# Attention masks as bf16 products on TensorE; maxima and exponentials read from PSUM

## The chip, the cores and the metric

One core of a Trainium2 chip runs the whole program. The metric is device time in microseconds (us); lower is better. The engines are TensorE (PE in the profile, its weight loads PEld), VectorE (DVE), ScalarE (ACT), GpSimd (POOL) and SyncE (SP), which issues most transfers. Matrix products write to PSUM, 8 banks of 512 fp32 numbers for each of 128 partitions.

## The reference

Three blocks of width 1024 run over one sequence of 256 tokens in fp32: sparse attention with a feed-forward part, a gated linear recurrence (HGRN) with one, and a block with gated linear attention and latent attention side by side, then a third feed-forward part. The change touches two softmaxes.

```python
# block 1: 16 heads of 64; each query keeps its best 64 keys
score = jnp.where(causal[None], score, -jnp.inf)
_, sel = lax.top_k(score, topk)
valid = sel <= t_pos[None, :, None]
logits = jnp.einsum('bqgrd,bqkgd->bqgrk', qg, k_sel) * (ATT_HEAD_DIM ** -0.5)
logits = jnp.where(valid[:, :, None, None, :], logits, -jnp.inf)
p = jax.nn.softmax(logits, axis=-1)
o = jnp.einsum('bqgrk,bqkgd->bqgrd', p, v_sel)
...
# block 3: 8 heads of 128 + 64 (rope)
s = jnp.where(mask[None, None], s, -jnp.inf)
p = jax.nn.softmax(s, axis=-1)
return jnp.einsum('bhqk,bkhd->bqhd', p, v)
```

## The kernel before

Weights come as 168 tiles of 128x2048 fp32 through a ring of six (`load`, L322, on SyncE). ScalarE rounds each to a high half (`hi`, L330), GpSimd subtracts to get the low half (`lo`, L334), and TensorE multiplies high and low halves in three passes (`mm3`, L350 to L352). A tile's place is free for the next load when TensorE has used it. ScalarE splits tiles between its other work, in the order that the code gives (`hi_until`); it splits none while it runs the attention loop.

Both attention stages use the same three loops, one for each engine: `attend_pe`, `attend_act`, `attend_dve`. They work on pairs of heads: eight pairs in the 16-head stage (`dsa_pe`), four in the 8-head stage (`mla_pe`). The logits of one head are 128x384: queries 0 to 127 against 128 keys, and queries 128 to 255 against all 256. The two heads of pair i lie in PSUM banks 2(i mod 2) and 2(i mod 2)+1, so that two pairs have room. For a pair:

- TensorE computes the logits (`logits`: L677, L678 in the 16-head stage; L1839, L1841 in the 8-head one). All these products have fp32 operands.
- VectorE adds the mask while it copies both heads from PSUM to the SBUF buffer `lg[i % 3]` (L761, 128x768), which frees the banks (`lg_free`). Then it takes the maxima (L767, L768) and multiplies them by minus the scale (L771).
- ScalarE applies the exponential in place in `lg`, four passes with sums (L736).
- VectorE takes reciprocals (L777) and normalises (L783).
- TensorE transposes six blocks (L721) to banks 4 and 5; ScalarE copies them to `pts` (L744); TensorE multiplies by the values (L685 to L687, or L1849 to L1851) into bank 6 or 7; ScalarE and VectorE split the output into a high and a low half (L858 and L951, or L1897 and L1951).

Every engine runs its instructions in the order of the code and waits on semaphores. TensorE's order is: logits of pairs 0 and 1; then for each i: wait for `lg_free` of pair i, logits of pair i+2, wait for the normalised pair i (`pn_ready`), transposes of pair i, value products of pair i-1. ScalarE's: exponentials 0 and 1; then copy i, output i-1, exponentials i+2. VectorE's: mask addition and maxima of i+2, normalise i+1, output half of i-1.

The mask of the 16-head stage, `sbias`, is made by VectorE after the selection of the best keys (L941, L946); the logits of pairs 0 and 1 are computed while that selection runs. The mask of the 8-head stage, `mbias`, is a constant that GpSimd writes in the setup (L409 to L412).

## Time and profile before

| | us |
|---|---|
| median of 3 runs | 1232.85 (1232.03 to 1233.91) |
| profiled execution | 1234.36 |
| its span, first to last instruction | 1232.2 |
| TensorE busy | 1112.5 (90%) |
| GpSimd busy | 829.6 (67%) |
| ScalarE busy | 551.1 (45%) |
| VectorE busy | 471.4 (38%) |
| mask additions, L761: 8 of 0.947 and 4 of 0.956 | 11.4 |
| mean granted clock of TensorE | 0.956 |

A busy share is a mean over stages that have different limits, so the timelines of the two stages tell more than the table. A timeline row gives start, duration, engine, line, operation and operands; [x <- y] is idle time before it and what ended that. The granted clock is 1.00 for TensorE's 2.4 GHz and 0.50 for 1.2 GHz. An fp32 product shows as two records.

### The profile page before, as it was taken

Reading aid. Unit: us, or ns where it says so; the run is one execution under the profiler, and the core shown is the slowest. Engines: PE = TensorE matmul, PEld = TensorE weight load, DVE = VectorE, ACT = ScalarE, POOL = GpSimd, SP = SyncE. Lnnn points to the kernel's source line nnn. Section 1 sums busy time; section 2 is a strip of 40 time slices with the busy share of each in tenths; the row PEclk is TensorE's granted clock in tenths of the full one; section 3 lists DMA queues with packets and bytes.
Section 4 is the critical chain, followed back from the end, with each engine's and each line's share of the span. In section 5 each row is a group of like instructions: output and inputs, shape, how many; then the busy total and the mean of one; then the engine's idle time right before and its main releaser. Section 6 shows DMA issues by size and latency. Waiting matters only on the chain.

```text
span 1232.2 us, 15620 instructions
## 1 busy us (share of the span) xinstructions
PE 1112.5 (90%) x6548; PEld 961.9 (78%) x6548; DVE 471.4 (38%) x854; ACT 551.1 (45%) x742; POOL 829.6 (67%) x299
## 2 busy tenths in 40 slices
PE   4675999999999966599999998999988898999997
PEld 4564787888889964477888888999988797788886
DVE  7559531114450779952111023260127525111102
ACT  3354544444335455444443425455563533543430
POOL 5243249978849757546987956978486274798880
PEclk9876999999999986699999999999998999999999
DMA  7210165555446530046555544554434143655540
GB/s 260 104 57 1 38 255 189 199 174 182 160 164 234 184 104 1 2 158 230 176 191 185 176 170 155 183 178 165 144 130 171 46 161 137 222 188 187 176 166 35
DMA packets 27952, 185.88 MB, mean 151 GB/s; under 512 B 3630, under 2 KB 4060, under 8 KB 6380
## 3 DMA queue, kind: packets, MB, share of 16 engines
q1 hardware_dynamic: 26156, 178.60, 41.2%
q10 hardware_dynamic: 1728, 6.29, 1.5%
q8 instruction: 52, 0.85, 0.3%
q14 instruction: 16, 0.13, 0.0%
HBM read 183.83 MB, written 1.05 MB: 150 GB/s over the span
## 4 chain that ended last, share of the span: by engine, by line
PE 78%; DVE 14%; ACT 3%; POOL 2%; issue 1%; DMA 1%; DVEq 0%
PE ps L350 24%; PE ps L352 24%; PE ps L351 24%; POOL wl L334 2%; DVE arena L1448 2%; DVE arena L468 1%; DVE arena L1449 1%; ACT wh L330 1%; PE ps L1114 1%; PE ps L1841 1%; DVE arena L1463 1%; PE ps L979 1%; DMA stage<-in_tiles 1%; DVE arena L783 1%; DVE arena L924 1%
## 5 line engine op out<-in xcount | busy, mean ns | idle before, releaser
L334 POOL TENSOR_TENSOR wl<-stage,wh 128x2048 fp32r<-128x2048 f32 x168 | 773.9, 4636 | 306.9 <-ACT wh L330 306.8
L330 ACT ACTIVATE wh<-stage 128x2048 fp32r<-128x2048 f32 x168 | 319.1, 1911 | 95.3 <-DMA stage<-in_tiles 94.3
L350 PE MATMUL ps<-wh,xh 128*128 128x512 f32 (+1 forms) x808 | 306.9, 380 | 18.2 <-POOL wl L334 5.9
L352 PE MATMUL ps<-wh,xl 128*128 128x512 f32 (+1 forms) x808 | 301.2, 373 | 0.0
L351 PE MATMUL ps<-wl,xh 128*128 128x512 f32 (+1 forms) x808 | 301.0, 372 | 0.0
L350 PEld LDWEIGHTS ps<-wh,xh 128*128 128x128 f32 x808 | 155.3, 192 | 48.4 <-issue 5.7
L350 PE MATMUL ps<-xh,wh 128*128 128x256 f32 x628 | 180.0, 287 | 8.6 <-DVE xl L1911 4.1
L351 PE MATMUL ps<-xl,wh 128*128 128x256 f32 x628 | 178.8, 285 | 0.0
L352 PE MATMUL ps<-xh,wl 128*128 128x256 f32 x628 | 178.7, 285 | 0.0
L352 PEld LDWEIGHTS ps<-wh,xl 128*128 128x128 f32 x808 | 155.2, 192 | 26.1
L351 PEld LDWEIGHTS ps<-wl,xh 128*128 128x128 f32 x808 | 155.6, 193 | 24.7 <-issue 0.5
L350 PEld LDWEIGHTS ps<-xh,wh 128*128 128x128 f32 x628 | 121.6, 194 | 10.7 <-DVE xl L1911 4.3
L1205 DVE TENSOR_TENSOR arena<-arena,ps 128x256 f32<-128x256 f32 x66 | 27.8, 421 | 251.3 <-ACT arena L1182 251.3
L351 PEld LDWEIGHTS ps<-xl,wh 128*128 128x128 f32 x628 | 121.7, 194 | 0.1
L352 PEld LDWEIGHTS ps<-xh,wl 128*128 128x128 f32 x628 | 121.7, 194 | 0.0
L350 PE MATMUL ps<-wh,hh 128*128 128x512 f32 x296 | 117.7, 398 | 0.0
L351 PE MATMUL ps<-wl,hh 128*128 128x512 f32 x296 | 117.0, 395 | 0.0
L352 PE MATMUL ps<-wh,hl 128*128 128x512 f32 x296 | 117.0, 395 | 0.0
L1182 ACT ACTIVATE arena<-ps 128x256 f32<-128x256 f32 x66 | 25.3, 383 | 186.9 <-PE ps L352 186.8
L352 PEld LDWEIGHTS ps<-wh,hl 128*128 128x128 f32 x296 | 55.6, 188 | 13.4
L351 PEld LDWEIGHTS ps<-wl,hh 128*128 128x128 f32 x296 | 55.6, 188 | 13.1
L350 PEld LDWEIGHTS ps<-wh,hh 128*128 128x128 f32 x296 | 55.6, 188 | 13.1
(338 smaller groups left out, 1136.9 us busy)
## 6 DMA issues: line engine op xcount, KB each, us to landing
stage<-in_tiles SPq DMA_DIRECT2D x168, 1024.0 KB, 4.9
arena<-in_ln_g ACTq DMA_DIRECT2D x4, 512.0 KB, 3.5
arena<-in_ln_b ACTq DMA_DIRECT2D x4, 512.0 KB, 4.7
x_res<-in_x SPq DMA_DIRECT2D x1, 1024.0 KB, 5.1
out<-x_res SPq DMA_DIRECT2D x4, 256.0 KB, 2.0
arena<-in_pre_mix_norm ACTq DMA_DIRECT2D x1, 512.0 KB, 7.9
arena<-in_post_mix_norm ACTq DMA_DIRECT2D x1, 512.0 KB, 3.7
arena<-in_pre_ffn_norm ACTq DMA_DIRECT2D x1, 512.0 KB, 5.0
```

The costliest lines, as they stand in the source:

```text
L330: nc.scalar.activation(wh[:, ring(n), :], stage[:, ring(n), :], ACT.Copy).then_inc(hi_done, 1)
L334: nc.gpsimd.tensor_tensor(wl[:, ring(n), :], stage[:, ring(n), :], wh[:, ring(n), :].bitcast(F32), ALU.subtract).then_inc(lo_done, 1)
L350: mm(out_, lh, rh, start=start, stop=False, skip_group_check=skip)
L351: mm(out_, lh, rl, start=False, stop=False, skip_group_check=skip)
L352: return mm(out_, ll, rh, start=False, stop=stop, skip_group_check=skip)
L468: V.scalar_tensor_tensor(out=x, in0=n, scalar=-part, in1=x, op0=ALU.mult, op1=ALU.add).then_inc(dve_step.sem, dve_step.up())
L783: ins = V.tensor_scalar(x, x, small[:, w:w + 1], None, ALU.mult)
L924: V.scalar_tensor_tensor(out=score[:, c0:c1], in0=x, scalar=w, in1=score[:, c0:c1], op0=ALU.mult, op1=ALU.add).then_inc(scored.sem, scored ...
L979: last = nc.tensor.transpose(ps[:, bank + b, k * P:(k + 1) * P], src[:, t, c:c + P], ident[:])
L1182: nc.scalar.activation(silu_g[:, p % 2, t, :], ps[:, pair_bank(G, p, t), 0:256], ACT.Silu).then_inc(s_done.sem, s_done.up())
L1205: V.tensor_tensor(hp[:, p % 2, t, :], silu_g[:, p % 2, t, :], ps[:, pair_bank(G, p, t), 256:512], ALU.mult).then_inc(h_mul.sem, h_mul.up())
L1448: V.tensor_tensor(y[:, :, 0:d], k_[:, :, 0:d], e[:, :, 0:d], ALU.mult)
```

## The change

The masks `mbias` and `sbias` become bf16, and GpSimd writes a bf16 copy of the identity matrix, `identb`, in the setup. The logits are no longer closed sums: TensorE adds the mask to them in PSUM as a product of `identb` and the mask (`masked` in `attend_pe`), four products for a pair of heads. `attend_dve` loses the mask addition; its maxima are read from PSUM. ScalarE's exponentials read PSUM and write `lg`. The semaphore `lg_free` is gone. TensorE's logits of pair i+2 wait for `p_ready`, the end of the exponentials of pair i. The logits of pairs 0 and 1 are both issued ahead of the first mask; in the 16-head stage TensorE waits for `sbias` between them and the masks.

```diff
@@ -177,8 +177,9 @@
-        mbias = sb("mbias", [P, 3 * P])
-        sbias = sb("sbias", [P, 3 * P])
+        mbias = sb("mbias", [P, 3 * P], BF16)
+        sbias = sb("sbias", [P, 3 * P], BF16)
+        identb = sb("identb", [P, P], BF16)
@@ -402,6 +403,8 @@
+            pool.wait_ge(consts.sem, consts.now())
+            nc.gpsimd.tensor_copy(identb[:], ident[:])
@@ -674,9 +677,9 @@
-                    mm(ps[:, b, 0:P], qt[:, i, 0:P], kpad[:, gr, e, 0:P], start=True, stop=True)
-                    last = mm(ps[:, b, P:3 * P], qt[:, i, P:T], kpad[:, gr, e, :], start=True, stop=True)
-                return last
+                    mm(ps[:, b, 0:P], qt[:, i, 0:P], kpad[:, gr, e, 0:P], start=True, stop=False, skip_group_check=True)
+                    mm(ps[:, b, P:3 * P], qt[:, i, P:T], kpad[:, gr, e, :], start=False, stop=False,
+                       skip_group_check=True)
@@ -686,7 +689,10 @@
-            attend_pe(pe, HEADS // 2, logits, weighted)
+            logits(0)
+            logits(1)
+            pe.wait_ge(sel_done.sem, sel_done.due(pe, 2))
+            attend_pe(pe, HEADS // 2, logits, sbias, weighted)
@@ -696,7 +702,14 @@
-        def attend_pe(pe, pairs, logits, weighted):
+        def attend_pe(pe, pairs, logits, bias, weighted):
+            def masked(i):
+                for e in range(2):
+                    b = 2 * (i % 2) + e
+                    mm(ps[:, b, 0:P], identb[:], bias[:, 0:P], start=False, stop=True, skip_group_check=True)
+                    last = mm(ps[:, b, P:3 * P], identb[:], bias[:, P:3 * P], start=False, stop=True, skip_group_check=True)
+                last.then_inc(lg_ps.sem, lg_ps.up())
+
@@ -707,11 +720,12 @@
             for i in range(2):
-                logits(i).then_inc(lg_ps.sem, lg_ps.up())
+                masked(i)
             for i in range(pairs):
                 if i + 2 < pairs:
-                    pe.wait_ge(lg_free.sem, lg_free.due(pe))
-                    logits(i + 2).then_inc(lg_ps.sem, lg_ps.up())
+                    pe.wait_ge(p_ready.sem, p_ready.due(pe))
+                    logits(i + 2)
+                    masked(i + 2)
@@ -732,8 +746,8 @@
-                        x = lg[i % 3][:, e, c0:c1]
-                        ins = nc.scalar.activation(x, x, ACT.Exp, bias=small[:, at + 4:at + 5], scale=scale,
+                        x, y = lg[i % 3][:, e, c0:c1], ps[:, 2 * (i % 2) + e, c0:c1]
+                        ins = nc.scalar.activation(x, y, ACT.Exp, bias=small[:, at + 4:at + 5], scale=scale,
@@ -751,17 +765,10 @@
-        def attend_dve(dve, pairs, scale, bias, outputs):
-            def masked(i):
+        def attend_dve(dve, pairs, scale, outputs):
+            def largest(i):
                 dve.wait_ge(lg_ps.sem, lg_ps.due(dve))
-                x = lg[i % 3]
-                if i >= 3:
-
-                    dve.wait_ge(pt_ps.sem, pt_ps.seen(dve) + i - 2)
-                V.tensor_tensor(x, ps[:, 2 * (i % 2):2 * (i % 2) + 2, 0:3 * P],
-                                bias.unsqueeze(1).to_broadcast([P, 2, 3 * P]), ALU.add
-                ).then_inc(lg_free.sem, lg_free.up())
-                dve.wait_ge(lg_free.sem, lg_free.now())
+                x = ps[:, 2 * (i % 2):2 * (i % 2) + 2, 0:3 * P]
...
@@ -1850,7 +1856,9 @@
-            attend_pe(pe, MH // 2, logits, weighted)
+            logits(0)
+            logits(1)
+            attend_pe(pe, MH // 2, logits, mbias, weighted)
```

In `mla_pe` the three products of a logit block change their start and stop flags in the same way.

TensorE, 8-head stage, before, from the last logits of pair 1 to the transposes of pair 0 (L1839 and L1841 are the logits, L721 the transposes; `m_d`, `m_a` and the like are semaphores):

```order
L1839 MATMUL ps<-arena 128x256
L1841 MATMUL ps<-arena 128x256 x2
L1839 MATMUL ps<-arena 128x128 [waits lg_free]
L1841 MATMUL ps<-arena 128x128 x2
...
L721 MATMUL ps<-ident,arena 128x128 [waits pn_ready]
L721 MATMUL ps<-ident,arena 128x128 x5
```

The same place after (the logits are now L1845 and L1848, the masks L709 and L710, the transposes L735):

```order
L1845 MATMUL ps<-arena 128x256
L1848 MATMUL ps<-arena 128x256 x2
L709 MATMUL ps<-mbias,identb 128x128
L710 MATMUL ps<-mbias,identb 128x256
...
L1845 MATMUL ps<-arena 128x128 [waits p_ready]
L1848 MATMUL ps<-arena 128x128 x2
...
L709 MATMUL ps<-mbias,identb 128x128
L710 MATMUL ps<-mbias,identb 128x256
L735 MATMUL ps<-ident,arena 128x128 [waits pn_ready]
L735 MATMUL ps<-ident,arena 128x128 x5
```

The masks of pairs 0 and 1 (two rows twice for each pair) stand behind the logits of both, the logits of pair 2 wait for `p_ready` instead of `lg_free`, and their masks stand between them and the transposes of pair 0. In the 16-head stage the order is the same, with a wait for `sel_done` at the first mask.

VectorE, 16-head stage, one turn of its loop before (L761 mask addition, L767 and L768 maxima, L777 reciprocals, L783 normalising):

```order
L761 TENSOR_TENSOR arena<-ps,sbias 128x768 [waits lg_ps]
L767 TENSOR_REDUCE small<-arena 128x2 [waits lg_free]
L768 TENSOR_REDUCE small<-arena 128x2
L771 TENSOR_SCALAR small<-small 128x4 [waits dve_step]
L777 RECIPROCAL small<-small 128x4 [waits p_ready]
L783 TENSOR_SCALAR arena<-arena,small 128x128 [waits dve_step]
```

And after:

```order
L774 TENSOR_REDUCE small<-ps 128x2 [waits lg_ps]
L775 TENSOR_REDUCE small<-ps 128x2
L778 TENSOR_SCALAR small<-small 128x4 [waits dve_step]
L784 RECIPROCAL small<-small 128x4 [waits p_ready]
L790 TENSOR_SCALAR arena<-arena,small 128x128 [waits dve_step]
```

The addition is gone, the maxima read PSUM and wait for TensorE's masks themselves, and the rest keeps its order.

## Rows read from the trace of the kernel before

**Rows 1.** Page, chain that ended last, by engine, as shares of the span.

```profile
PE 78%; DVE 14%; ACT 3%; POOL 2%; issue 1%; DMA 1%; DVEq 0%
```

**Rows 2.** Timeline, VectorE, one period, 16 heads: start, duration, [idle before].

```profile
122.03 0.95 DVE L761 TENSOR_TENSOR arena<-ps,sbias 128x768 f32<-128x768 f32 x1
123.02 0.42 DVE L767 TENSOR_REDUCE small<-arena 128x2 f32<-128x256 f32 x1
...
125.60 0.95 DVE L761 TENSOR_TENSOR arena<-ps,sbias 128x768 f32<-128x768 f32 x1
```

**Rows 3.** Timeline, TensorE, the same period.

```profile
122.64 0.43 PE L685 MATMUL ps<-arena 128*64 128x128 f32 x2
...
123.72 0.49 PE L677 MATMUL ps<-arena 128*128 128x128 f32 x2
124.04 0.60 PE L678 MATMUL ps<-arena 128*128 128x256 f32 x2
...
124.70 0.60 PE L678 MATMUL ps<-arena 128*128 128x256 f32 x2
125.41 0.87 PE L721 MATMUL ps<-ident,arena 128*128 128x128 f32 x6
126.21 0.43 PE L685 MATMUL ps<-arena 128*64 128x128 f32 x2
```

**Rows 4.** Timeline, TensorE, head of the 16-head attention.

```profile
106.57 0.80 PE L677 MATMUL ps<-arena 128*128 128x128 f32 x2 [12.39 <-DVE arena L761]
...
108.44 1.06 PE L678 MATMUL ps<-arena 128*128 128x256 f32 x2
111.05 1.54 PE L721 MATMUL ps<-ident,arena 128*128 128x128 f32 x6 [1.55 <-DVE arena L783]
...
114.68 0.82 PE L721 MATMUL ps<-ident,arena 128*128 128x128 f32 x6
```

**Rows 5.** Timeline, ScalarE, its first exponential.

```profile
107.80 0.40 ACT L736 ACTIVATE arena<-arena,small 128x128 f32<-128x128 f32 x1 [19.11 <-DVE small L771]
```

**Rows 6.** Chain that ended last, end of the 16-head attention: start, us, what.

```profile
131.40 1.87 ACT arena L736 x8
```

**Rows 7.** Timeline, TensorE, the 8-head attention.

```profile
957.65 0.46 PE L1839 MATMUL ps<-arena 128*128 128x128 f32 x2 [2.07 <-DVE small L1948]
...
965.59 0.38 PE L1839 MATMUL ps<-arena 128*128 128x128 f32 x2
...
974.10 0.82 PE L721 MATMUL ps<-ident,arena 128*128 128x128 f32 x6
...
979.95 0.87 PE L721 MATMUL ps<-ident,arena 128*128 128x128 f32 x6
```

**Rows 8.** Timeline, VectorE, first mask addition of the 8-head attention.

```profile
961.86 0.96 DVE L761 TENSOR_TENSOR arena<-ps,mbias 128x768 f32<-128x768 f32 x1 [4.35 <-PE ps L1841]
```

**Rows 9.** Timeline, ScalarE, first exponential of the 8-head attention.

```profile
964.10 0.40 ACT L736 ACTIVATE arena<-arena,small 128x128 f32<-128x128 f32 x1 [5.66 <-DVE small L771]
```

**Rows 10.** Timeline, TensorE, another wait.

```profile
51.81 0.47 PE L350 MATMUL ps<-wh,xh 128*128 128x512 f32 x1 [2.18 <-DVE xl L890]
```

**Rows 11.** Windows: length, busy us of each engine, granted clock, DMA share, GB/s.

```profile
53.00:56.30 3.30, 3.30 (x9) 2.54 (x8) 3.23 (x6) 0.35 (x1) 2.87 (x1) 0.50 0.22 92
926.80:933.50 6.70, 5.59 (x26) 5.59 (x27) 6.37 (x8) 0.09 (x1) 5.31 (x1) 0.50 0.16 66
```

**Rows 12.** Groups by form, ScalarE: busy us, mean ns; idle before.

```profile
L1182 ACT ACTIVATE arena<-ps 128x256 f32<-128x256 f32 x66 | 25.3, 383 | 186.9 <-PE ps L352 186.8
L1339 ACT ACTIVATE arena<-arena 128x256 f32<-128x256 f32 x48 | 20.0, 416 | 39.9 <-POOL arena L1408 39.9
```

**Rows 13.** Timeline, TensorE, neighbouring products of 256 columns.

```profile
985.25 0.27 PE L352 MATMUL ps<-xh,wl 128*128 128x256 f32 x1
985.37 0.28 PE L350 MATMUL ps<-xh,wh 128*128 128x256 f32 x1
```

**Rows 14.** Waits of TensorE: us in total, times, longest.

```profile
PE ps L350 <- POOL wl L334: 5.9, 6, 1.5
```

More of the change, by code:

```diff
@@ L291, in build @@
         q_rot, qt_ps, qt_done, sel_done = signals("q_rot qt_ps qt_done sel_done")
-        lg_ps, lg_free, nmx_ready, p_ready, pn_ready, pt_ps, pts_done, ot_ps, oh_done = signals(
-            "lg_ps lg_free nmx_ready p_ready pn_ready pt_ps pts_done ot_ps oh_done")
+        lg_ps, nmx_ready, p_ready, pn_ready, pt_ps, pts_done, ot_ps, oh_done = signals(
+            "lg_ps nmx_ready p_ready pn_ready pt_ps pts_done ot_ps oh_done")
         s_done, h_mul, h_ready = signals("s_done h_mul h_ready")
@@ L726, in attend_pe @@
             value(pairs - 1)
-            lg_free.skip(pe, 2)
+            p_ready.skip(pe, 2)
         def attend_act(act, pairs, scale, outputs):
@@ L784, in normalised @@
                 ins.then_inc(pn_ready.sem, pn_ready.up())
-            masked(0)
-            masked(1)
+            largest(0)
+            largest(1)
             normalised(0)
@@ L790, in attend_dve @@
                 if i + 2 < pairs:
-                    masked(i + 2)
+                    largest(i + 2)
                 if i + 1 < pairs:
@@ L796, in attend_dve @@
                     outputs(i - 1)
-            pt_ps.skip(dve, pairs)
             dve.wait_ge(oh_done.sem, oh_done.due(dve))
@@ L952, in outputs @@
                 ).then_inc(x_ready.sem, x_ready.up())
-            attend_dve(dve, HEADS // 2, HD ** -0.5, sbias[:], outputs)
+            attend_dve(dve, HEADS // 2, HD ** -0.5, outputs)
         def dsa_pool(pool):
@@ L1838, in logits @@
                         y = slice(t * P, (t + 1) * P)
-                        mm(ps[:, b, c0:c1], qn[:, h, y], kn[:, h, 0:c1 - c0], start=True, stop=False)
+                        mm(ps[:, b, c0:c1], qn[:, h, y], kn[:, h, 0:c1 - c0], start=t == 0, stop=False,
+                           skip_group_check=True)
                         for x in range(2):
-                            last = mm(ps[:, b, c0:c1], rr[:, x, h // 4, y], kp[x][:, h % 4, 0:c1 - c0],
-                                      start=False, stop=x == 1)
-                return last
+                            mm(ps[:, b, c0:c1], rr[:, x, h // 4, y], kp[x][:, h % 4, 0:c1 - c0],
+                               start=False, stop=False, skip_group_check=True)
             def weighted(i, e, pt, _):
@@ L1952, in outputs @@
                 ).then_inc(x_ready.sem, x_ready.up())
-            attend_dve(dve, MH // 2, (MN + MR) ** -0.5, mbias[:], outputs)
+            attend_dve(dve, MH // 2, (MN + MR) ** -0.5, outputs)
             dve.wait_ge(gates_done.sem, 4)
```

## The prediction

> **What bounds the kernel now.** I read three views in this order: the chain that ended last, then the timelines of the two attention stages engine by engine, then the granted clock around waits. The chain is TensorE for 78% of the span and VectorE for 14% [rows 1], so a VectorE instruction is worth something only in a stage where the chain runs over VectorE. The change touches two short stages: the 16-head attention (about 105.6 to 138.4 us) and the 8-head one (957.65 to about 984.9).
>
> In the **16-head stage** VectorE sets the pace. One pair of heads is one turn of its loop: from one mask addition (L761) to the next is 125.60 - 122.03 = 3.57 us, and the addition holds 0.99 of it, up to the start of the maxima [rows 2]. TensorE is close behind. Its turn is the value products (122.64 to 123.72, 1.08 us), the logits of the pair two further on (123.72, their last row ends at 124.70 + 0.60 = 125.30), and the six transposes (125.41 to 126.21, 0.80) [rows 3]. Records overlap: the row at 123.72 is 0.49 long and the next starts at 124.04, 0.17 before its end. With as much behind the last one, TensorE's own work is 1.08 + 1.41 + 0.80 = 3.29 us of the 3.57.
>
> In the **8-head stage** TensorE sets the pace up to the second group of transposes: the logits of the first two pairs run from 957.65 to 965.59, 3.97 us a pair, and those of the third pair follow without a pause [rows 7]. Behind 974.10 the chain goes over ScalarE (copy, output, exponentials) and VectorE to the last transposes at 979.95 [rows 7].
>
> **The change part by part.**
>
> *Mask addition on VectorE, removed.* 12 instructions of 0.95 us. In the 16-head stage six of them stand in the steady loop: VectorE's turn falls from 3.57 to 2.58 us. In the 8-head stage only the first one (961.86) is on the way to the exponentials [rows 8].
>
> *Masks on TensorE, added.* Each pair gets four bf16 products, 128, 256, 128 and 256 columns. The trace has no bf16 product. Neighbouring single-pass products of 256 columns start 0.12 us apart [rows 13]; a 128-column one cannot cost more than that and hardly less than half. A pair costs 2 x (0.06 + 0.12) = 0.36 to 4 x 0.12 = 0.48; I take 0.40, since every one also loads the identity. At the half clock I take 0.80. The Trainium skill ("TensorE: Matmul & The Clock Gate", section "Wait — 56ns, not 53.3ns?") measures 55.6 ns for 128 bf16 columns. By it a pair would cost about 0.33 us, an estimate, and the six masks on the path would be 0.4 us cheaper together.
>
> *Maxima and exponentials out of PSUM.* A ScalarE pass over 128x256 takes 383 ns from PSUM and 416 from SBUF, of different functions [rows 12]. I take 0.03 us less for each of four exponentials in a pair, 0.13 a pair, with bounds 0 and 0.4. L761 reads PSUM and takes 0.95 us for 768 elements, no more per element than the maxima out of SBUF (0.42 for 256) [rows 2], so the maxima stay the same; bounds -0.05 and +0.15 a pair. The Trainium skill ("VectorE: DVE Perf Modes", section on the TRN2 errata) gives VectorE a fixed term of 58 cycles from SBUF and 120 from PSUM. That would be 0.13 us more for the two maxima of a pair, a rule against this change; the row of L761 shows nothing of it, and the sum would move by under 0.3 us.
>
> *The wait that is exchanged.* This is the heart of it. Before, TensorE's logits of pair i+2 wait for the mask addition of pair i, which empties the bank. Now the bank is read by the exponentials, and the wait is for them. What queues behind it on TensorE, in order: those logits, their masks, the transposes of pair i, and the value products.
>
> 8-head stage. The masks of pair 0 now stand behind the logits of both first pairs. So pair 0's maxima start not at 962.85 (961.86 plus 0.99 [rows 8]) but at 965.59 + 0.40 (its masks) + 0.2 (time to the end of the last product) = 966.2. That is 3.35 later, and the first exponential moves from 964.10 [rows 9] to 967.45. The pair's exponentials take 1.87 us [rows 6], so they end at 969.3. Logits of pair 2 start at 969.36 instead of 965.59: +3.77. Two masks on the way to the second transposes add 0.80. Second transposes: 974.10 + 4.57 = 978.67. Behind them the order is unchanged, over ScalarE, and the mask of the last pair is already done; the third transposes have over a microsecond of room. Less 0.13 for the exponentials of the first pair and of the last: **+4.3 us**.
>
> 16-head stage, head. Logits of two pairs lie ready long before; only their masks wait for the selection. TensorE had been idle for 12.39 us and is slow: six transposes take 1.54 us where they take 0.87 later [rows 3, 4]. The masks of pair 0, 0.80 plus 0.2, end where the addition ended (106.57 [rows 4]), so the first exponential stays at 107.80 [rows 5]: removed and added work cancel. But logits of pair 2, which filled TensorE's idle time from 106.57 to 109.50 [rows 4], now wait for the exponentials, 107.80 + 1.87 = 109.7. They then need 2.6 at the slow clock and their masks 0.80: first transposes at 113.1 instead of 111.05, ended at 114.4. Logits 1.41 and masks 0.40 at full clock: second transposes at 116.3 instead of 114.68 [rows 4], +1.6. If the clock rises sooner, because TensorE now works without a pause from 109.7, it is +0.9. I take +1.4.
>
> 16-head stage, loop. TensorE's turn is 3.29 + 0.40 = 3.69 against 3.57. VectorE has 2.6, so TensorE now sets the pace. The way over ScalarE is shorter: transposes to value products 0.80, to the output 1.19, to the exponentials 0.44, these 1.87, less the 0.91 from the next transposes to their copy, makes 3.4. Four turns: **+0.5** (bounds +0.2 and +1.4). From the sixth transposes on the end runs over ScalarE as before, through the last pair's exponentials at 131.40 [rows 6]: -0.1. Stage sum 1.4 + 0.5 - 0.1 = **+1.8**.
>
> *The clock.* In the 8-head stage TensorE now stands idle from about 966.2 to 969.36, 3.2 us. A wait of 2.18 us at 49.6 [rows 10] was followed by 3.3 us at clock 0.50 with TensorE busy throughout; behind a longer one TensorE was busy 5.59 us of a stretch at 0.50 [rows 11]. The wait of 2.07 us before 957.65 [rows 7] brought no fall. Half of the busy time is lost: 1.7 or 2.8 us. The logits behind the gap are all on the path. I take **+2.0**.
>
> *Setup.* GpSimd copies the identity once to bf16, and waits once for it; it stands idle for 9 us before its first weight tile, so this costs nothing. If it were not hidden it would be 0.5 us.
>
> Sum: 4.3 + 1.8 + 2.0 = 8.1 us. The profiled execution took 1234.36 us (span 1232.2), 1.5 above the median of 1232.85; it would become 1242.5, and the median **1241.0**. What follows either stage is work released by its last output, on all engines, so the delay arrives whole at the end.
>
> **Rivals.**
> *The clock does not fall.* For it: the wait of 2.07 us. Against: the wait of 2.18 us, and this one is 3.2. Sum 6.1: 1239.0.
> *Bf16 masks cost TensorE more than any row shows*, through changes between fp32 and bf16 or weight loads that are not hidden, 0.8 a pair. Nothing in the trace speaks for it. Twice the mask cost on eight masks of the path is +3.2: 1244.2.
> *The delay is taken up behind the 8-head stage* (the other side). If the weight pipeline set the pace there, a later start would only shorten TensorE's waits for it. The 6.3 us of that stage vanish, and +1.8 is left, 1234.7, within what counts as no change. It decides only if TensorE then waits over 6 us for low halves of weights; all such waits together are 5.9 us, the longest 1.5 [rows 14], and the splitting on ScalarE is queued behind the attention, so it starts later too.
> *VectorE's freed time carries through*: if masks cost TensorE nothing, the turn is 3.4 by ScalarE, four turns give -0.7, and the stage ends at +0.6; the rest stays: 1239.8. It lies inside the range.
>
> **How the numbers follow.** Forecast with the fall of the clock 0.60, no fall 0.24, dearer masks 0.08, taken up behind 0.05, the freed time 0.03. The range: low end with no fall, head +0.9 and cheap exponentials, 4.0 + 1.0 = 5.0, so 1237.5; high end with the clock at 2.8, head 1.6, loop +1.4 and masks at 0.48, about 11.5, so 1244.5. A measurement of this kernel tells 0.2% (2.5 us) from no change. Slower by more: 0.92. Within: 0.06, nearly all from the fourth case. Faster: 0.02.
>
> **What the profile after would show.** A gap on TensorE of about 3.2 us behind the first two masks of the 8-head stage, ended by the exponentials of ScalarE; clock 0.50 behind it; second transposes 4.6 us later than before, or more by the clock. In the 16-head stage the logits of pair 2 start near 109.7, transposes come 3.7 us apart and VectorE has idle time in each turn. The prediction is wrong if transposes come under 3.5 us apart, if that gap is under 2 us, or if the end of a stage moves and the span does not.

## The result

Before: 1233.03 us, median of 6 (1231.87 to 1233.99). After: 1237.35 us, median of 6 (1236.75 to 1239.8). The ratio is 1.0036, 95% interval 1.0026 to 1.0047: the changed kernel is 4.3 us slower. The direction was forecast, the size was not: 1241.0 was predicted, with a range from 1237.5, and the median lies just under it. One execution further on, in experiment two, took 6107.85 us, and the ratio there leaves it out.

The profiled execution of after took 1239.8 us (span 1237.5), the slowest of its six. Against the profiled execution of before (1234.36) that is 5.4 us. All of it lies in the two attention stages:

| stretch of the two traces | before | after |
|---|---|---|
| start to the mask `sbias` | 105.52 | 105.50 |
| `sbias` to the next weight product | 32.90 | 34.14 |
| from there to the first logits of the 8-head stage | 819.23 | 819.09 |
| 8-head stage, to the weight product behind it | 27.26 | 31.46 |
| from there to the end of the span | 247.3 | 247.3 |

So the 16-head stage cost 1.2 us, the 8-head stage 4.2, and nothing was taken up behind either. The setup, 105.50 us to the mask against 105.52, cost nothing, as forecast.

The page of after, its busy times and its chain by engine (the chain answers to [rows 1]):

```profile
PE 1111.2 (90%) x6596; PEld 962.1 (78%) x6596; DVE 460.6 (37%) x842; ACT 547.9 (44%) x742; POOL 829.6 (67%) x300
...
PE 78%; DVE 13%; ACT 4%; POOL 3%; issue 1%; DMA 0%; DVEq 0%
```

VectorE is busy for 10.8 us less than before (471.4), and the kernel is slower: VectorE went down in the chain by a single percent.

The timeline of TensorE in the head of the 16-head stage of after (start, duration, operation, [idle before <- what ended it]; it answers to [rows 4]). L709 and L710 are the masks, L680 and L681 the logits, L735 the transposes:

```profile
105.56 0.29 PE L709 MATMUL ps<-sbias,identb 128*128 128x128 bf16 x1 [11.15 <-DVE sbias L952]
105.64 0.42 PE L710 MATMUL ps<-sbias,identb 128*128 128x256 bf16 x1
...
109.51 0.80 PE L680 MATMUL ps<-arena 128*128 128x128 f32 x2 [2.50 <-ACT arena L750]
...
112.88 1.49 PE L735 MATMUL ps<-ident,arena 128*128 128x128 f32 x6
...
116.29 0.82 PE L735 MATMUL ps<-ident,arena 128*128 128x128 f32 x6
```

The logits of pair 2 start 2.9 us later than before (106.57): they wait for ScalarE's exponentials. At half the clock they and their masks need 3.37 us up to the transposes (109.51 to 112.88).

One turn of the steady loop of after, TensorE (it answers to [rows 3]):

```profile
119.86 0.82 PE L735 MATMUL ps<-ident,arena 128*128 128x128 f32 x6
...
121.68 0.49 PE L680 MATMUL ps<-arena 128*128 128x128 f32 x2
...
123.10 0.22 PE L709 MATMUL ps<-sbias,identb 128*128 128x128 bf16 x1
123.15 0.27 PE L710 MATMUL ps<-sbias,identb 128*128 128x256 bf16 x1
123.26 0.22 PE L709 MATMUL ps<-sbias,identb 128*128 128x128 bf16 x1
...
123.43 0.82 PE L735 MATMUL ps<-ident,arena 128*128 128x128 f32 x6
```

A turn is 123.43 - 119.86 = 3.57 us, to the hundredth what it was before, when VectorE set it. It is now TensorE's own work without a pause: 1.82 (transposes and value products), 1.42 (logits), 0.33 (four masks, 123.10 to 123.43). In the same turn VectorE (it answers to [rows 2]) waits for the masks:

```profile
120.06 0.42 DVE L774 TENSOR_REDUCE small<-ps 128x2 f32<-128x256 f32 x1 [0.89 <-PE ps L710]
120.40 0.68 DVE L775 TENSOR_REDUCE small<-ps 128x2 f32<-128x512 f32 x1
```

That 0.89 us of idle time is what became of the 0.99 us of the mask addition. The maxima take from PSUM what they took from SBUF (0.42).

The 8-head stage of after, TensorE (it answers to [rows 7]); L1845 and L1848 are the logits:

```profile
958.73 0.46 PE L1845 MATMUL ps<-arena 128*128 128x128 f32 x2 [2.07 <-DVE small L1956]
...
966.67 0.22 PE L709 MATMUL ps<-mbias,identb 128*128 128x128 bf16 x1
...
970.23 0.49 PE L1845 MATMUL ps<-arena 128*128 128x128 f32 x2 [2.74 <-ACT arena L750]
...
979.51 0.82 PE L735 MATMUL ps<-ident,arena 128*128 128x128 f32 x6
```

and ScalarE's first exponential, which answers to [rows 9]:

```profile
968.46 0.37 ACT L750 ACTIVATE arena<-ps,small 128x128 f32<-128x128 f32 x1 [8.94 <-DVE small L778]
```

From the first logits to the second transposes it is 20.78 us, before 16.45. The two masks' products of pair 0 stand behind the logits of both pairs, the first exponential comes 9.73 us after the stage's start instead of 6.45, and TensorE stands for 2.74 us. Behind it TensorE runs at full clock: from the first transposes to the second it is 979.51 - 974.60 = 4.91 us, 0.65 for the transposes, 3.93 for a pair's logits and 0.33 for its masks.

### The profile page after: what moved, and what is told of

It is laid out like the page before. It is cut to its first block, busy times and chain, and to the rows that moved or that the text cites. A ratio compares the mean times of both kernels' runs of the same rounds, so it can differ in the third digit from the quotient of the medians.

```text
span 1237.5 us, 15699 instructions
## 1 busy us (share of the span) xinstructions
PE 1111.2 (90%) x6596; PEld 962.1 (78%) x6596; DVE 460.6 (37%) x842; ACT 547.9 (44%) x742; POOL 829.6 (67%) x300
## 4 chain that ended last, share of the span: by engine, by line
PE 78%; DVE 13%; ACT 4%; POOL 3%; issue 1%; DMA 0%; DVEq 0%
PE ps L351 24%; PE ps L353 23%; PE ps L352 23%; POOL wl L335 3%; DVE arena L1454 2%; DVE arena L471 1%; DVE arena L1455 1%; ACT wh L331 1%; PE ps L1120 1%; PE ps L1848 1%; DVE arena L1469 1%; PE ps L735 1%; PE ps L985 1%; ACT arena L750 1%; PE ps L681 1%
## 5 line engine op out<-in xcount | busy, mean ns | idle before, releaser
L353 PEld LDWEIGHTS ps<-wh,hl 128*128 128x128 f32 x296 | 55.6, 188 | 13.4
L352 PEld LDWEIGHTS ps<-wl,hh 128*128 128x128 f32 x296 | 55.6, 188 | 13.1
L351 PEld LDWEIGHTS ps<-wh,hh 128*128 128x128 f32 x296 | 55.6, 188 | 13.1
```

Of the source, the lines that this page charges most:

```text
L351: mm(out_, lh, rh, start=start, stop=False, skip_group_check=skip)
L352: mm(out_, lh, rl, start=False, stop=False, skip_group_check=skip)
L353: return mm(out_, ll, rh, start=False, stop=stop, skip_group_check=skip)
```

## The experiments

Ratios are against the kernel before, run on the same chip in the same series, with 95% intervals; its medians there were 1233.37 (one to four), 1233.96 (five to eight), 1234.01 (nine to twelve) and 1234.13 us (thirteen to fifteen). A ratio is not the quotient of the medians: a few long executions move it and not them. The theory that they test (A): the loss is the exchanged wait and the place of the masks behind both pairs' logits, in two places, plus a slow clock of TensorE that may or may not follow the gap. What a trace shows of single stretches is one execution; the medians are over 5 to 12.

**One: where the masks of pair 0 stand.** The changed kernel, but in the 8-head stage the masks of a pair follow that pair's logits, so those of pair 0 come ahead of the logits of pair 1.

```
             logits(0)
+            masked(0)
             logits(1)
-            masked(0)
             masked(1)
```

> The changed kernel, but in the 8-head stage the masks of pair 0 stand right behind the logits of pair 0, ahead of those of pair 1. Theory A (the order of the masks behind both logit blocks makes the wait for the exponentials visible; nothing else costs much in this stage): pair 0's exponentials end about 965 to 966 relative to a stage start of 957.65, before TensorE is through with pair 1, so the gap of 2.7 us is gone; from the stage's first product to the second transposes 16.45 + 4 x 0.33 = 17.8 us against 20.8 in the changed kernel; time 3.0 us below the changed kernel, about 1.3 above the kernel before. Rival B (the exchanged wait itself costs, wherever the masks stand): a gap of over 1 us stays, and the time is less than 1.5 us below the changed kernel.

Measured: 1234.61 us, median of 12; ratio 1.0016 (1.0004 to 1.0028). Its TensorE timeline in the 8-head stage:

```profile
972.65 0.27 PE L713 MATMUL ps<-mbias,identb 128*128 128x256 bf16 x1
972.76 0.39 PE L1887 MATMUL ps<-arena 128*128 128x128 f32 x2
```

The masks of pair 1 end and the logits of pair 2 follow without a gap: the exponentials of pair 0 are done in time. From the first logits to the second transposes the trace has 19.44 us. Of these 1.67 are a slow clock at the start of the stage, behind the wait of 2.05 us ahead of it; the first logits to the first transposes take 14.52 us, where in before, with three pairs' masks added, they would take 12.85. Less that it is 17.77, against 20.78 in after and 17.8 expected: the place of the masks is worth 3.0 us in the trace. In time it is 3.1 us by the medians (1.2 over before instead of 4.3) and some 2.3 by the ratios, in which the longest execution weighs. So the order of four small products cost several times what their execution does. The profiled execution was that longest one, 1242.23 us; the rest of its loss lies ahead of the stage, of the kind shown at thirteen below.

**Two and three: one stage at a time.** Two has the change in the 16-head stage alone, three in the 8-head stage alone; the other stage keeps VectorE's fp32 masks and the old wait.

> The change in the 16-head stage alone; the 8-head stage as before, with its fp32 mask and the addition on VectorE. Theory A (the stages add up, as their spans in the two traces say): +1.2 us against the kernel before, +0.2 to +1.5 depending on when the clock rises at the head of the stage, and 4.2 below the changed kernel. Rival B (in most executions the head of this stage gains, since TensorE is at full clock earlier than in the profiled one, and the measured 4.3 us are the 8-head stage alone): 0.0 or below.

> The change in the 8-head stage alone; the 16-head stage as before, with its fp32 mask and the addition on VectorE. Theory A: +4.2 us against the kernel before. If the clock fell behind the gap in most executions, as forecast: +6. If the delay were taken up behind the stage: under +1.

Measured: two 1233.97 us, ratio 1.0003 (0.9994 to 1.0012), with the stage 1.2 us longer in its trace (34.13), so the interval holds both no loss and the 1.2 us that were expected; three 1241.81 us, ratio 1.0059 (1.0045 to 1.0073). Three is slower than the whole change. Its trace, in windows (length, busy us of each engine, granted clock, DMA share, GB/s):

```profile
958.10:961.50 3.40, 3.40 (x12) 2.86 (x12) 0.00 (x0) 0.08 (x1) 3.24 (x1) 0.51 0.41 171
961.50:970.50 9.00, 6.32 (x42) 5.50 (x41) 2.28 (x6) 1.71 (x9) 1.25 (x1) 1.00 0.00 0
971.70:975.10 3.40, 3.40 (x13) 2.96 (x12) 0.07 (x1) 0.42 (x2) 0.00 (x0) 0.50 0.00 0
```

The clock fell twice to 1.2 GHz (0.50), with TensorE busy throughout: once behind the wait of 2.07 us ahead of the stage, once behind the 2.74 us gap. The stage took 34.80 us, which is 31.46 and twice 1.67. That accounts for this trace. Why the median of three lies over that of the whole change, which has the same gap, is not shown.

**Four and seven: the gap filled.** Twelve unread fp32 products of 128 columns into bank 4 behind the masks of pairs 0 and 1; four is the whole change so filled, seven the 8-head stage alone.

```
+            for _ in range(12):
+                mm(ps[:, 4, 0:P], ident[:], ident[:], start=True, stop=True)
```

> The changed kernel with twelve fp32 products of 128 columns (identity by identity, into bank 4, read by nobody) in the gap of the 8-head stage, so that TensorE is busy for 2.6 of its 2.7 us. If the clock falls behind the gap in most executions (the forecast), this takes away 1.7 to 2.8 us. If it does not fall, as in the profiled execution of the changed kernel: within 0.3 us of it.

> The change in the 8-head stage alone, with twelve fp32 products that nobody reads in its gap. Theory C (the clock falls behind the 2.7 us gap in many executions, each time for 3.4 us or more): 1 to 2.5 us below the kernel that changes the 8-head stage alone, so about +5 against the kernel before. Rival D (the clock is the same with and without the gap): no difference to it.

Measured: four 1237.73 us, ratio 1.0038 (1.0025 to 1.0051), the same as the changed kernel; its trace shows the filler and the second transposes at 20.78 us, as in after:

```profile
964.95 2.84 PE L753 MATMUL ps<-ident 128*128 128x128 f32 x24
967.86 0.49 PE L1887 MATMUL ps<-arena 128*128 128x128 f32 x2
```

Seven 1238.49 us, ratio 1.0031 (1.0019 to 1.0043): 0.0028 or 3.4 us under three. The filler takes nothing away in the whole change, and in the 8-head stage alone as much as two falls cost. But it stands behind only one of three's two waits: the fall ahead of the stage it cannot have prevented, and seven's trace has none there either. So the 3.4 us are not shown to be the filler's alone.

**Five: TensorE kept warm ahead of the 16-head stage, first try.** Three unread products after each of seven rounds of the selection, and twelve behind the first masks.

> The changed kernel, with products nobody reads on TensorE in the 16-head stage: three fp32 products of 128 columns after each of seven rounds of the selection, and twelve in the wait behind the first masks. TensorE then has its full clock at the first mask. Theory A (the +1.6 us at the head of this stage is the slow clock under the logits of pair 2, which now stand on the path): first mask to second transposes 7.9 us instead of 10.7, and the time 2.8 us below the changed kernel. Rival (the head is set by the exponentials, not by the clock): under 1 us.

Measured: 1237.35 us, ratio 1.0048 (1.0028 to 1.0068), in two groups of executions, about 1236.7 and 1244. The trace shows that it didn't do what was meant:

```profile
91.25 4.85 PE L690 MATMUL ps<-ident 128*128 128x128 f32 x42
102.78 0.29 PE L715 MATMUL ps<-sbias,identb 128*128 128x128 bf16 x1 [6.68 <-DVE sbias L1000]
```

The first products were used up by 96.1, TensorE then stood for 6.7 us, and the masks ran at half clock as before. The twelve behind them brought the full clock for the logits of pair 2 and held these up by their own length; from the first mask to the second transposes it is 10.05 us instead of 10.73, where 7.9 was expected. The question is left to nine.

**Six: the exchanged wait alone.** The kernel before, masks in fp32 on VectorE, but TensorE's logits of pair i+2 wait for the exponentials of pair i.

```
-                    pe.wait_ge(lg_free.sem, lg_free.due(pe))
+                    pe.wait_ge(p_ready.sem, p_ready.due(pe))
```

> The kernel before with the exchanged wait alone: masks in fp32 and added by VectorE, but TensorE's logits of pair i+2 wait for the exponentials of pair i instead of the mask addition, in both stages. Theory A (the wait alone is nearly hidden in the 8-head stage, where TensorE works on pair 1 until 0.4 us before the exponentials of pair 0 end; what costs there is that the masks of pair 0 stand behind the logits of pair 1): +0.4 us from the 8-head stage and +0.4 from the head of the 16-head one, together +0.8 against the kernel before. Rival B (the wait itself is the loss): +3 or more.

Measured: 1234.13 us, ratio 1.0003 (0.9995 to 1.0012). In its trace the 16-head stage is 34.00 us long (before 32.90) and the 8-head stage 27.79 (27.26):

```profile
109.44 0.79 PE L681 MATMUL ps<-arena 128*128 128x128 f32 x2 [15.28 <-ACT arena L787]
...
966.78 0.49 PE L1890 MATMUL ps<-arena 128*128 128x128 f32 x2 [0.26 <-ACT arena L787]
```

The wait alone makes nearly the whole 1.2 us of the 16-head stage, in the head, and an eighth of the 8-head stage's 4.2. There the masks' place makes the rest, as experiment one says from the other side.

**Eight: the changed kernel once more.**

> The changed kernel itself, beside these. Theory A without a fall of the clock: 5.4 us above the kernel before, as the spans of the two stages say (1.2 and 4.2). With a fall behind the gap in most executions, 6 to 7.5 above. 4.3, as measured first, if the head of the 16-head stage costs less in most executions than in the profiled one. The trace shows which stretch of the 8-head stage has which clock.

Measured: 1238.58 us, ratio 1.0034 (1.0021 to 1.0047). This time its trace has the fall that was predicted, behind the same 2.74 us gap (windows, as above, both behind the gap):

```profile
968.50:971.90 3.40, 3.40 (x13) 2.99 (x13) 0.02 (x1) 0.38 (x2) 0.00 (x0) 0.54 0.00 0
972.00:980.00 8.00, 8.00 (x59) 7.29 (x59) 3.74 (x13) 3.23 (x10) 0.00 (x0) 0.99 0.01 2
```

The second transposes come at 22.45 us instead of 20.78: one fall costs 1.67 us. Seven traces have the gap unfilled (after, three, five, eight, and nine, thirteen and fourteen below); four show the fall (three, eight, thirteen, fourteen), and the second transposes then come 1.67 us later each time. The two with the filler show none. The wait of 2.0 to 2.07 us ahead of the stage was unfilled in fourteen traces, and the clock fell behind it in three (one, three and fifteen), again for 1.67 us each time.

**Nine: the 16-head stage at full clock.** The changed kernel; behind the logits of pairs 0 and 1 TensorE computes 30 unread products, waits for the first part of `sbias`, computes 17 more, and 10 behind the masks.

> The changed kernel, and TensorE no longer rests while the selection of the 16-head stage runs: behind the logits of pairs 0 and 1 it computes 30 unread fp32 products of 128 columns into bank 4, waits for the first part of sbias, computes 17 more, and 10 more behind the masks of pairs 0 and 1. Theory A (the price of the head of the 16-head stage is the slow clock under work that was moved behind sbias): at full clock the masks of pair 0, the logits of pair 2, their masks and the first transposes take 0.33 + 1.41 + 0.33 + 0.87 us instead of 0.64 + 2.6 + 0.64 + 1.54, so from the first mask to the second transposes it is about 8.2 us instead of 10.7, and the kernel lies 2.5 us under the changed kernel: 1.8 over before, ratio 1.0015. Rival B (ScalarE and VectorE set the head once the logits wait for the exponentials): under 1 us is gained, ratio 1.0030.

Its TensorE timeline:

```profile
105.30 0.23 PE L716 MATMUL ps<-sbias,identb 128*128 128x128 bf16 x1 [0.59 <-DVE sbias L1001]
...
108.95 0.49 PE L681 MATMUL ps<-arena 128*128 128x128 f32 x2 [0.58 <-ACT arena L791]
...
110.69 0.82 PE L774 MATMUL ps<-ident,arena 128*128 128x128 f32 x6
...
113.30 0.88 PE L774 MATMUL ps<-ident,arena 128*128 128x128 f32 x6
```

From the first mask to the second transposes it is 8.00 us, against 10.73 in after; 8.2 was expected. The stage takes 31.46 us, 2.7 less than after and 1.4 less than before. For the stage theory A holds: the price of its head is the slow clock. It does not show that TensorE is the better place for the masks, since before's head is at half clock; eleven below, which fills the same wait with the masks on VectorE, has 32.96 us, but its clock falls again behind a wait of 2.90 us ahead of the first transposes. The time does not follow: three executions took 1235.7 to 1236.2 us (1.1 to 2.9 under the changed kernel's two medians, 1237.35 and 1238.58), four took 1242.3 to 1244.1; median 1242.29, ratio 1.0049 (1.0027 to 1.0072). No execution of the kernel before (82) or of the changed kernel (11) took over 1240 us; 1 of 12 did in one, 4 of 9 in five and 4 of 7 here.

**Thirteen and fourteen: traces of the slower executions of nine.** The same kernel, twice.

> The kernel of e9_full_clock_16 once more, for the trace alone. Its seven executions fell into two groups, three of 1235.7 to 1236.2 us and four of 1242.3 to 1244.1, at the same mean clock (0.958 to 0.961); only one of the first group has a trace. Theory A (with a waiting TensorE kept busy the stage itself takes its 8.0 us from the first mask to the second transposes, and the 6 to 8 us come in at another place): in a slow execution the 16-head stage is again about 31.4 us long and the whole difference lies outside it. Rival B (the unread products outlast the wait for sbias in some executions and hold the masks up): the stage itself is 6 us or more longer.

> The same kernel as e13_full_clock_again, for a second chance of a trace from the slower group. Expected as there.

They took 1243.27 and 1250.57 us. In thirteen the 16-head stage is 31.45 us long, as in nine, and the loss is in the third block, ahead of the 8-head stage (825.27 us between the stages instead of 818.47), as theory A of that expectation said. The timeline of all engines at the same place, of nine and then of thirteen (DVE is VectorE; POOL L336 is GpSimd's splitting of weight tiles):

```profile
939.23 0.69 DVE L1994 TENSOR_TENSOR arena<-arena 128x512 f32<-128x512 f32 x1
939.61 4.79 POOL L336 TENSOR_TENSOR wl<-stage,wh 128x2048 fp32r<-128x2048 f32 x1 [9.66 <-ACT wh L332]
939.95 4.47 DVE L1996 COPY small<-small 128x2 f32<-128x2 f32 x1
```

```profile
937.69 9.52 POOL L336 TENSOR_TENSOR wl<-stage,wh 128x2048 fp32r<-128x2048 f32 x2 [8.46 <-ACT wh L332]
937.77 0.69 DVE L1992 TENSOR_TENSOR arena<-ps,trig_t 128x512 f32<-128x512 f32 x1
938.50 4.36 DVE L1994 TENSOR_TENSOR arena<-arena 128x512 f32<-128x512 f32 x1
...
942.89 4.34 DVE L1996 COPY small<-small 128x2 f32<-128x2 f32 x1
```

In nine GpSimd started at 939.61, when L1994 was already running, and one VectorE instruction was held. In thirteen it started at 937.69, ahead of L1994, and two in a row were held, 4.36 and 4.34 us, where they take 0.69 and 0.17 (0.17 is that copy in fifteen's trace). L1992, which reads PSUM, was not. TensorE then waited:

```profile
947.29 0.80 PE L352 MATMUL ps<-wh,xh 128*128 128x512 f32 x1 [5.34 <-DVE small L1996]
```

5.34 us instead of 0.61, and its clock fell to 0.50 behind that. Why GpSimd started sooner shows some 15 us ahead, at the wait of [rows 11], here of nine and then of thirteen:

```profile
925.58 0.58 PE L352 MATMUL ps<-xh,wh 128*128 128x256 f32 x1 [4.16 <-DVE xl L1967]
```

```profile
924.36 0.39 PE L352 MATMUL ps<-xh,wh 128*128 128x256 f32 x1 [2.89 <-DVE xl L1967]
```

In nine GpSimd was still splitting tiles when L1967 (two inputs from SBUF) began, and it took 2.76 us; in thirteen the tiles were done, and it took 1.49. TensorE then waited 2.89 us instead of 4.16, its mean clock in the 6.7 us from 924.4 was 0.75 instead of 0.54 (from 924.5), the next tiles came sooner, and so did the collision. All three traces of long executions (one, thirteen, fourteen) have the wait of 2.89 us; the other eleven traces with this wait unfilled, before's and after's among them, have 4.12 to 4.16. So in the traces the shorter executions are those in which TensorE waits longer here. Ten, below, has the same by experiment. In fourteen the same happened, and besides the other rival came true: the selection ended with `sbias` ready at 105.04, while the 17 unread products stood ahead of the masks:

```profile
104.63 6.70 PE L691 MATMUL ps<-ident 128*128 128x128 f32 x34 [4.27 <-DVE sbias L996]
111.16 0.22 PE L716 MATMUL ps<-sbias,identb 128*128 128x128 bf16 x1
```

Here the two instructions that write `sbias` came behind each other in 0.8 us, after GpSimd's tiles; in after and in nine they were held for 4.0 and 4.6 us. The filler was sized for that case and delayed the masks by 6.1 us.

**Ten to twelve: waits filled in the kernel before.** Ten: 16 unread products in the wait of 4.13 us behind which the clock is 0.50 [rows 11], and 8 in the wait ahead of the 8-head stage. Eleven: also the products of nine. Twelve: also the masks of pairs 3, 5 and 7 of the 16-head stage on TensorE.

> The kernel before, masks on VectorE, with unread products in two waits of TensorE in the third block: 16 fp32 products of 128 columns in the wait of 4.13 us at 923.8, and 8 in the wait of 2.07 us ahead of the 8-head attention. Theory A (the granted clock falls behind a wait of TensorE and not by itself): the 6.7 us at clock 0.50 from 926.8, in which TensorE is busy for 5.59, become full clock and give back 2.8 us: ratio 0.9977, about 1230.6. Rival B (the clock falls there whatever TensorE does, or what follows is bound by the splitting of weights): nothing is gained, ratio 1.000; products that outlast the wait cost up to 1 us.

> As e10_two_waits_filled, and the products of e9_full_clock_16 in the wait for the selection too (30, 17, and 4 behind the logits of pair 1), masks on VectorE. Theory A (slow clock in the head of the 16-head stage costs the kernel before something too): the first transposes take 0.87 instead of 1.54 us, and the second ones come 0.7 to 1.5 us sooner: ratio 0.9968. Rival B: VectorE's mask additions set the head, 0.3 us or less is gained: 0.9975.

> As e11_all_filled, and the masks of pairs 3, 5 and 7 of the 16-head stage come from TensorE in bf16 (maxima and exponentials of these pairs from PSUM), all others from VectorE; the 8-head stage keeps its fp32 masks on VectorE. Theory A (before, the loop is VectorE's with 3.57 us a pair; with all masks on TensorE it is TensorE's with 3.57; shared, neither has them all): TensorE has 3.29 and 3.62 us in turn, so the transposes come 3.4 to 3.5 us apart and some 0.5 us are gained: ratio 0.9964. Rival B (the wait for the exponentials, exchanged for these pairs, costs TensorE what VectorE gains): no gain, 0.9968 or more.

Measured: 1237.35, 1237.4 and 1237.16 us; ratios 1.0029 (1.0019 to 1.0039), 1.0030 (1.0019 to 1.0041), 1.0038 (1.0023 to 1.0053). All three lose where a gain was expected, and the trace of ten tells why. First the wait that it fills and the next one, in before:

```profile
927.91 0.58 PE L350 MATMUL ps<-xh,wh 128*128 128x256 f32 x1 [4.13 <-DVE xl L1911]
...
946.92 0.50 PE L350 MATMUL ps<-wh,xh 128*128 128x512 f32 x1 [0.44 <-DVE small L1940]
```

Then ten:

```profile
926.80:933.50 6.70, 6.70 (x58) 6.70 (x57) 6.06 (x9) 0.01 (x1) 2.19 (x1) 1.00 0.46 157
...
943.70:950.60 6.90, 4.36 (x10) 3.46 (x11) 2.49 (x1) 0.00 (x0) 2.46 (x1) 0.51 0.01 2
```

```profile
946.24 0.79 PE L352 MATMUL ps<-wh,xh 128*128 128x512 f32 x1 [5.59 <-DVE small L1997]
```

The first row is the stretch of [rows 11]: the clock is 1.00 now. But TensorE's next tiles came sooner, GpSimd started its pair of tiles sooner (936.40), and VectorE's same two instructions fell behind it (3.55 and 4.34 us). TensorE waited 5.59 us where it had waited 0.44, and the slow clock came there. Up to the start of that wait 2.7 us were gained (805.39 us behind the 16-head stage instead of 808.06), and more was given back, 4.5 us net between the stages. Eleven and twelve have the same wait, 5.56 and 5.61 us. Eleven's own question, whether the slow clock in the head of the 16-head stage costs the kernel before something too, got no clean answer: its second transposes come 9.16 us after `sbias`, as in before, with the clock fallen again.

**Fifteen: masks shared.** The kernel before, and the masks of pairs 3, 5 and 7 of the 16-head stage on TensorE.

> The kernel before, and the masks of pairs 3, 5 and 7 of the 16-head stage from TensorE in bf16, their maxima and exponentials from PSUM; all other masks on VectorE, no unread products. Theory A (the loop is bound by VectorE before and by TensorE with all masks there; shared it is bound by neither all the time, as the trace of e12_all_filled_mixed shows with transposes 3.29 and 3.59 us apart in turn): stage 0.5 us shorter than before's 31.85 from the logits of pair 2 to the next weight product, time 0.5 us under before, ratio 0.9996, which such a measurement cannot tell from 1. Rival B (the gain in e12 hangs on the filled wait): stage 31.8 or longer, ratio 1.0000 or more.

Measured: 1233.16 us, median of 12, beside 1234.13 for before; ratio 0.9999 (0.9986 to 1.0012), no change. Its TensorE timeline:

```profile
113.38 0.82 PE L770 MATMUL ps<-ident,arena 128*128 128x128 f32 x6
116.62 0.82 PE L770 MATMUL ps<-ident,arena 128*128 128x128 f32 x6
120.20 0.87 PE L770 MATMUL ps<-ident,arena 128*128 128x128 f32 x6
123.50 0.82 PE L770 MATMUL ps<-ident,arena 128*128 128x128 f32 x6
```

The transposes come 3.24, 3.58 and 3.30 us apart instead of 3.57. From the second transposes to the next weight product it is 22.85 us against 23.74, 0.9 less; 0.6 of that goes in the first interval (4.23 instead of 3.63), where the masks of pair 3 run in the cold head. What is left, 0.3 us, no such measurement can tell. Of the versions with masks on TensorE this one and two cannot be told from before; none is faster.

## Why the prediction was right and where it failed

*8-head stage, +4.3.* The forecast held: +4.33 at the second transposes, +4.20 at the stage's end. Its three parts held as well: masks behind both pairs' logits, ScalarE's exponentials behind them, two masks on the path. The masks were sized too dear and half of that came back elsewhere. They cost 0.33 us a pair, not 0.40 (the logits of the first two pairs end and the masks of pair 0 begin at 966.67, those of pair 1 at 967.00), three times 0.07 less on the way to the second transposes; the logits of pair 2 took 4.03 us behind the gap (970.23 to 974.26) where they take 3.92 without one. The exponentials took 1.73 us; 1.74 was forecast. By the Trainium skill ("TensorE: Matmul & The Clock Gate", section "Wait — 56ns, not 53.3ns?"), 55.6 ns for 128 bf16 columns, the masks would take 0.33 us, and the trace agrees. Its other rule that was weighed, VectorE's longer fixed term from PSUM ("VectorE: DVE Perf Modes", the TRN2 errata), would show in the maxima; they take 0.42 us from either memory, so the measurement decides against it here.

*The gap, 3.2 us.* It was 2.74: the prediction let it begin behind pair 0's masks and forgot that those of pair 1 fill 0.33 of it, and the exponentials are shorter by 0.13, as the same text had said. 3.2 less 0.33 and 0.13 is 2.74.

*The clock, +2.0.* This is the failed step. It was written as the likely case (0.60) and sized between one half-clock stretch and a longer one. Measured: 1.67 us in four traces of seven, nothing in the other three, after's among them, and no gain of the median from filling the gap in the whole change (four against after). Over the seven traces that is 1.0 us, an estimate, where 2.0 was put into the sum. Whether the clock falls behind a gap of this length differs from one execution to the next, and so it does behind the 2.07 us wait ahead of the stage: none in before [rows 7], a fall in three traces of fourteen. The rows of before held one wait of 2.18 us with a fall and one of 2.07 us without; from two single cases a full cost was put on the likeliest case. Its rival, no fall, gave 1239.0 and was nearer. Without this term the sum is 6.1 us, and the two profiled executions, which show no fall, differ by 5.4; the loop and the tail below make that difference.

*16-head head, +1.4.* Measured +1.6 at the second transposes in the two profiled executions (10.79 against 9.16 us after `sbias`); over five traces with the changed stage the mean is 10.55 (10.33 to 10.79), over four with the old one 9.13 (8.89 to 9.42), so +1.4. Six has 10.54 with the exchanged wait alone: the wait makes it, not the masks. And it hangs on the clock: nine, at full clock, has 8.05.

*16-head loop, +0.5.* Measured 0.00: 3.57 us before and after. TensorE's own work without masks is 3.24, not 3.29, and the masks are 0.33, not 0.40; of 3.69 there remain 3.57. That this equals the old period to the hundredth is chance; the engine that sets it did change. The mark that was set, "wrong if transposes come under 3.5 us apart", was not reached. The rival of dearer bf16 masks, 0.8 us a pair, falls with the same 0.33.

*Tail, -0.1.* Measured -0.4: from the sixth to the last transposes it is 5.23 us against 5.60. The last pair's exponentials are shorter by 0.14 and start 0.22 sooner behind the sixth transposes (2.21 instead of 2.43). The output pass of ScalarE stands ahead of them in both; they follow its start by 0.28 us where it was 0.44, and why is not shown.

*Taken up behind the 8-head stage.* Fell, as weighed: 247.3 us from there to the end in all traces.

*The range.* Its ends do not come out of their own terms: 1232.85 + 5.0 is 1237.85, not 1237.5, and the terms named for the high end add up to some 10.6 us, not 11.5. By its sum the range would have begun further above the result.

*What stays open.* The stages sum to 5.4 us without a fall, as the two profiled executions show, and the medians differ by 4.3. The stretch ahead of `sbias`, whose work the change leaves alone but for the type of the masks, varied from 102.6 to 105.7 us between the traces, so two executions can differ by this much: in eight's trace it is 103.19, and though its stages cost 6.7 us with a fall, its span is 4.1 over before's. That this explains the 1.1 us of the medians is not shown.

## What to carry to other kernels

An engine that loses work gives time only until the next engine's turn: before taking 0.95 us from VectorE's loop, add what it puts on the neighbour's, here 3.24 + 0.33 us for TensorE, and compare with the old period. When a wait is moved to a later event of a chain, look first at the head of the stage, where nothing yet runs ahead: four small products behind two pairs' logits instead of one's cost 3.0 us in the traces, and their execution 0.33. And a filled wait or a warm clock in one place moves everything behind it; measure the whole kernel, since in ten to twelve, and in the traces of thirteen and fourteen, a collision of VectorE with GpSimd further on took more than had been gained.

## What the runs showed of the hardware

VectorE instructions that start while GpSimd subtracts a 128x2048 tile can be held until that tile is done: L1994 took 0.69 us or 4.36, a copy of two columns 0.17 or 4.34 to 4.59, the two writers of `sbias` 0.36 and 0.43 or 4.0 and 4.6. Others went through unhindered while a tile was being split: L1992, which reads PSUM, in its 0.69 us, and the selection's replacements in theirs, 0.28. With one more instruction held, at a place where TensorE waits for it, and the slow clock behind that wait, the stretch between the attention stages took 825.3 us in two traces of one kernel and 818.5 in a third. By the Trainium skill ("SBUF — State Buffer", section "SBUF: two separate sides") VectorE and GpSimd share a pair of ports that some VectorE instructions, those in a faster mode or with two inputs from SBUF, need and that one engine holds for a whole instruction; the traces agree, in that the held ones read SBUF alone and end about when a tile of GpSimd's does.

TensorE's granted clock fell to half (0.50) behind idle times of TensorE of 2.05 and 2.07 us in 3 traces of 14, and behind one of 2.74 us in 4 of 7, there in some executions and not in others of the same kernel. TensorE was busy afterwards each time, and such a fall cost 1.67 us.

A bf16 product between fp32 ones costs TensorE 0.055 us for 128 columns and 0.11 for 256, with no pause at the change of type. ScalarE's exponentials read from PSUM take 1.73 us a pair, from SBUF 1.87. VectorE's maxima take 0.42 and 0.68 us from either.
